# The expert stage of a diffusion layer: weights in whole-row chunks through twelve raw homes, products ordered gate, down of the neighbour, up

## The chip, the cores and the metric

The kernel runs on one core of a Trainium2 chip. The metric is the time of one execution on the device, in microseconds (us). The TensorE clock has two levels here, 1.2 and 2.4 GHz; the profile gives the granted clock as a share of the higher one.

## The reference, cut to what matters

One layer: a recurrent (RG-LRU) mixer over 1024 latent and 256 context tokens of width 1024, then a mixture of 16 experts where each expert chooses its 128 best tokens. The change touches the experts alone:

```python
xg = jax.vmap(lambda hb, ib: hb[ib])(h, idx)                    # 16 experts x 128 chosen rows x 1024
hid = jax.nn.silu(jnp.einsum('becd,edf->becf', xg, w_gate)) * jnp.einsum('becd,edf->becf', xg, w_up)
y = jnp.einsum('becf,efd->becd', hid, w_down) * gate[..., None].astype(h.dtype)   # f = 2048
return jax.vmap(lambda yb, ib: jnp.zeros((n, dm), yb.dtype).at[ib.reshape(-1)].add(yb.reshape(-1, dm)))(y, idx)
```

Everything is float32. Each expert's three weight matrices have 8 MB each, so 24 MB are read per expert, 384 MB in all, and each is used for 128 rows only.

## The kernel before, in words

The program is written out by hand for each engine, with semaphores between them. It has three stages: the mixer, the routing (output projection, softmax, top 128 of each expert), and the experts, which this document is about.

A float32 product is made of three: both operands are split into a rounded high part and the rest, the low part, and TensorE (PE) adds high times high, low times high and high times low. So each chunk of weights goes through a chain. SyncE (SP) loads it into a `raw` home of 1 MB (`load_chunk`). ScalarE (ACT) rounds it into `part_h` (`split` on ACT, recorded on the line of its helper `copy`, L498). VectorE (DVE) subtracts to get `part_l` (`split` on DVE, L980). PE does 12 matmuls of 128 columns of weights by 512 (L1218 to L1220 for gate and up, L1244 to L1246 for down), and `chunk_used` counts the chunks it has finished.

An expert has 24 chunks, with NS = 6 homes each for raw, high and low. The list `order` gives their sequence: two chunks of the neighbour's last down quarter, then for each quarter f of the 2048 hidden columns gate, gate, up, up, and behind them the two down chunks of quarter f-1. A gate or up chunk is four blocks of rows by 512 of the 2048 columns, so each partition gets four pieces of 2 KB; a down chunk is two pieces of 4 KB. `load_chunk` waits until the high and low parts of the chunk six earlier are made; ACT's `split` waits until PE has used the chunk six earlier.

For each quarter ACT takes silu of the gate product (`hidden`), DVE multiplies it by the up product into `hid` (`gate_up`, L987), PE transposes it (`turn_hidden`, L1228), and ACT and DVE split the transposed rows (`hidT_h`, `hidT_l` L991). Between experts PE transposes the next 128 rows (`turn_rows`, L1259), ACT scales and splits them (L683, L498), DVE makes `xgT_l` (L1009). DVE writes the expert's output `y_out` (L1000). GpSimd (POOL) scatters `y_out` with an adding DMA, then gathers the rows of the next expert. Each engine takes its instructions strictly in the written order, so one that waits holds all behind it.

Of the kernel before, what the change touches and what calls it, by code (L numbers as in the profile page):

```python
# [33 lines left out]
def program(nc, stack, x, c, ctx, c_ctx, ada_w, ada_b, norm_mix_g, norm_ffn_g, final_g, a_w_in, a_conv_w,  # L34
            a_conv_b, a_gate_wa, a_gate_ba, a_gate_wx, a_gate_bx, a_lambda, a_w_out, router_w,
            exp_w_gate, exp_w_up, exp_w_down, out):
    P = 128
# [99 lines left out]
    gate5_row = place("gate5_row", [P, D], F32, 195)  # L137
# [7 lines left out]
    NS = 6  # L145
    part_h = [place(f"part_h{s}", [P, 4 * HALF], F32R, 16 * s) for s in range(NS)]
    part_l = [place(f"part_l{s}", [P, 4 * HALF], F32R, 16 * s + 8) for s in range(NS)]
    raw = [place(f"raw{s}", [P, 4 * HALF], F32, 96 + 8 * s) for s in range(NS)]
    xg = place("xg", [P, D], F32, 146)
    xgT = place("xgT", [P, KD, P], F32, 150)  # L150
    xgT_h = place("xgT_h", [P, KD, P], F32R, 154)
    xgT_l = place("xgT_l", [P, KD, P], F32R, 158)
    act_g = [place(f"act_g{s}", [P, HALF], F32, 162 + 2 * s) for s in range(2)]
    hid = [place(f"hid{s}", [P, HALF], F32, 176 + 2 * s) for s in range(2)]
    hidT_h = [place(f"hidT_h{s}", [P, 4, P], F32R, 180 + 4 * s) for s in range(2)]
    hidT_l = [place(f"hidT_l{s}", [P, 4, P], F32R, 182 + 4 * s) for s in range(2)]
    y_out = place("y_out", [P, D], F32, 188)
# [24 lines left out]
    wg_v = exp_w_gate[0].rearrange("e (k p) f -> e p k f", p=P)  # L182
    wu_v = exp_w_up[0].rearrange("e (k p) f -> e p k f", p=P)
    wd_v = exp_w_down[0].rearrange("e (k p) f -> e p k f", p=P)
# [17 lines left out]
    raw_loaded = [stack.enter_context(nc.semaphore(f"raw_loaded{i}")) for i in range(NS)]  # L202
# [3 lines left out]
    fin_loaded = [stack.enter_context(nc.semaphore(f"fin_loaded{t}")) for t in range(NT)]  # L206
# [31 lines left out]
    order = [("d", 3, 0), ("d", 3, 1)]  # L238
    for f in range(NF):
        order += [("g", f, 0), ("g", f, 1), ("u", f, 0), ("u", f, 1)]  # L240
        if f:
            order += [("d", f - 1, 0), ("d", f - 1, 1)]
    CH = len(order)
    assert CH % NS == 0
    at = {key: i for i, key in enumerate(order)}

    used = lambda e, key: e * CH + at[key] - 1

    gate_at = lambda e, f: used(e, ("g", f, 1))
    up_at = lambda e, f: used(e, ("u", f, 1))  # L250
    down_at = lambda e, f: used(e + 1 if f == NF - 1 else e, ("d", f, 1))
    two_before = lambda e, f: (e, f - 2) if f >= 2 else (e - 1, f - 2 + NF)
# [6 lines left out]
    with nc.Block() as block:  # L259
# [3 lines left out]
        def _(sp):  # L263
# [108 lines left out]
            def load_chunk(e, i, first=False):  # L372
                kind, f, half = order[i]
                slot = i % NS
                if kind == "d":
                    e_of = e - 1 if f == NF - 1 else e
                    src = wd_v[bass.ds(e_of, 1), :, 4 * f + 2 * half:4 * f + 2 * half + 2, :]
                    dst = raw[slot][:].rearrange("p (k f) -> p k f", k=2)
                else:
                    src = (wg_v if kind == "g" else wu_v)[bass.ds(e, 1), :, 4 * half:4 * half + 4, f * HALF:(f + 1) * HALF]  # L380
                    dst = raw[slot][:].rearrange("p (k f) -> p k f", k=4)
                if not first:
# [8 lines left out]
            for i in range(2, 2 + NS):  # L391
                load_chunk(0, i, first=True)
            for t in range(NT - 2, NT):
                tile_stores(t, t % 2)

            for i in range(2 + NS, CH):
                load_chunk(0, i)
            with sp.Fori(1, E) as e:
                for i in range(CH):
                    load_chunk(e, i)  # L400

            for i in range(2):
                load_chunk(E, i)


            sp.wait_ge(sem["chunk_used"], E * CH)
            sp.dma_start(fin_g[:], row_of(final_g)).then_inc(sem["fin_g_loaded"], 16)
            sp.wait_ge(sem["scattered"], 16 * E)
            for t in range(NT):
                sp.dma_start(fin_in[:, t, :], x_scr[t * P:(t + 1) * P, :]).then_inc(fin_loaded[t], 16)  # L410
# [10 lines left out]
        def _(pool):  # L421
# [27 lines left out]
            for i in range(2, 2 + NS):  # L449
                slot = i % NS  # L450
                pool.wait_ge(sem["part_h_ready"], i - 1)
                nc.gpsimd.tensor_tensor(part_l[slot][:], raw[slot][:], part_h[slot][:].bitcast(F32), ALU.subtract
                                        ).then_inc(sem["part_l_ready"], 1)


# [28 lines left out]
            scatter(0, 1)  # L484
            with pool.Fori(1, E - 1) as e:
                pool.wait_ge(sem["gathered"], (e + 1) * 16)
                pool.wait_ge(sem["xgT_h_ready"], e + 1)
                gather(e + 1, sem["id_ready"], e + 1)
                scatter(e, e + 1)
# [6 lines left out]
        def _(act):  # L496
# [149 lines left out]
            def split(e, key):  # L646
                i = at[key]
                slot = i % NS
                uses = 0 if slot < 2 else 16
                act.wait_ge(raw_loaded[slot], e * (CH // NS * 16) + (i // NS) * 16 + uses)  # L650
                if not (isinstance(e, int) and e == 0 and i < 2 + NS):
                    act.wait_ge(sem["chunk_used"], e * CH + i - NS - 1)
                copy(part_h[slot][:], raw[slot][:]).then_inc(sem["part_h_ready"], 1)


            act.wait_ge(sem["gated_done"], 2 * NT)
            for key in order[2:2 + NS]:
                split(0, key)

            def hidden(e, f):  # L660

                act.wait_ge(sem["chunk_used"], gate_at(e, f))
                if not (isinstance(e, int) and e == 0 and f < 2):
                    act.wait_ge(sem["hid_ready"], e * NF + f - 1)
                nc.scalar.activation(act_g[f % 2][:], bank(2 * (f % 2)), ACT.Silu).then_inc(sem["silu_done"], 1)

            def turn_hidden(e, f):
                act.wait_ge(sem["hid_turned"], e * NF + f + 1)
                if not (isinstance(e, int) and e == 0 and f < 2):
                    act.wait_ge(sem["chunk_used"], down_at(*two_before(e, f)))  # L670
                copy(hidT_h[f % 2][:], bank(4 + f % 2)).then_inc(sem["hidT_h_ready"], 1)

            def expert(e, first=False):
                if not first:
                    split(e, ("d", 3, 0))
                    split(e, ("d", 3, 1))
                    turn_hidden(e - 1, 3)
# [10 lines left out]
                if not first:  # L688
                    act.wait_ge(sem["chunk_used"], up_at(e - 1, NF - 1))
                copy(xgT_h[:], xgT[:]).then_inc(sem["xgT_h_ready"], 1)  # L690
                for f in range(NF):
                    for key in (("g", f, 0), ("g", f, 1), ("u", f, 0), ("u", f, 1)):
                        if not (first and at[key] < 2 + NS):
                            split(e, key)
# [616 lines left out]
```

## Time and profile before

| | before |
|---|---|
| median of 3 runs | 1926.0 us (1923.76 to 1926.67) |
| the profiled execution | 1920.49 us, its span 1918.7 us |
| PE, VectorE, ScalarE busy, share of the span | 85%, 72%, 63% |
| granted TensorE clock, mean | 0.938 |
| moved by DMA | 511.08 MB, mean 266 GB/s |

How its rows are read. A row of the timeline has the start in us from the span's start, the duration in us, engine, line, operation, output<-inputs, shapes, the count of merged instructions, and in brackets the idle time of the engine before it with what ended it. A row of a table of windows has the stretch, its length, the busy us and instructions of PE, PEld (weight loads), DVE, ACT and POOL, then the granted clock, the busy share of the 16 DMA engines (a little over 1 where packets overlap), and GB/s. A row of waits has who waited on whom, the total, how often, and the longest. A queue's row has packets, MB, and the share of 16 engines' time that its packets took; q1 carries the loads of SP, q0 the gathers and scatters. A row of loads by line has the issue's min/median/max in ns, or the us from issue to landing.

### The profile page before, as it was taken

How to read it: one execution, taken by the hardware profiler on the slowest of the kernel's cores; microseconds unless marked ns; L12 is line 12 of the kernel's file. 1: busy time of each engine (PE TensorE's matmuls, PEld its weight loads, DVE VectorE, ACT ScalarE, POOL GpSimd, SP SyncE). 2: the span in 40 equal slices, each digit the busy share in tenths (PEclk: the TensorE clock that was granted, in tenths of full speed). 3: DMA queues.
4: the chain of work that ended last, by engine and by line, in shares of the span. 5: the costliest groups of instructions: out<-in, count | busy, mean ns of one | idle time of the engine just before them, and what ended most of it. 6: DMA issues, size and time to landing. Idle time of an engine off the chain costs nothing.

```text
span 1918.7 us, 21818 instructions
## 1 busy us (share of the span) xinstructions
PE 1638.6 (85%) x7524; PEld 1318.5 (69%) x7524; DVE 1388.0 (72%) x1044; ACT 1206.3 (63%) x1141; POOL 108.5 (6%) x125
## 2 busy tenths in 40 slices
PE   4999999946992098998989989989899899898992
PEld 1777777835882077877877777778777777787772
DVE  3778778764225757878878878788878788887784
ACT  4687887880224056767666667666675676666763
POOL 0300000000005000000000000000000000000000
PEclk7999999977995599999999999999999999999996
DMA  8234343324583159999999999999999999999995
GB/s 325 72 111 147 116 141 118 127 67 154 181 273 111 53 206 328 383 337 342 366 321 340 360 325 376 326 331 364 340 342 350 327 353 352 331 358 332 340 332 197
DMA packets 238469, 511.08 MB, mean 266 GB/s; under 512 B 10298, under 2 KB 56024, under 8 KB 236384
## 3 DMA queue, kind: packets, MB, share of 16 engines
q1 hardware_dynamic: 230944, 483.33, 70.0%
q0 software_dynamic: 7488, 27.27, 4.9%
q8 instruction: 22, 0.36, 0.1%
q14 instruction: 15, 0.12, 0.0%
HBM read 479.10 MB, written 31.46 MB: 266 GB/s over the span
## 4 chain that ended last, share of the span: by engine, by line
PE 76%; DVE 10%; ACT 7%; issue 2%; SPq 2%; DMA 2%; ACTq 0%; DVEq 0%; POOL 0%; POOLq 0%
PE psum L1218 13%; PE psum L1220 12%; PE psum L1219 12%; PE psum L1046 5%; PE psum L1048 5%; PE psum L1047 5%; PE psum L1244 5%; PE psum L1245 4%; PE psum L1246 4%; DVE part_l L980 4%; ACT xgT L683 2%; PE psum L1146 2%; PE psum L1147 2%; PE psum L1148 2%; ACT part_h L498 1%
## 5 line engine op out<-in xcount | busy, mean ns | idle before, releaser
L980 DVE TENSOR_TENSOR part_l<-raw,part_h 128x2048 fp32r<-128x2048 f32 x378 | 843.3, 2287 | 85.4 <-ACT part_h L498 85.4
L498 ACT ACTIVATE part_h<-raw 128x2048 fp32r<-128x2048 f32 x384 | 700.7, 1908 | 0.7 <-DMA raw<-in_exp_w_up_dram 0.7
L1218 PE MATMUL psum<-part_h,xgT_h 128*128 128x512 f32 x1024 | 415.6, 406 | 73.3 <-DVE part_l L980 68.7
L1219 PE MATMUL psum<-part_h,xgT_l 128*128 128x512 f32 x1024 | 406.3, 397 | 0.0
L1220 PE MATMUL psum<-part_l,xgT_h 128*128 128x512 f32 x1024 | 405.7, 396 | 0.0
L1218 PEld LDWEIGHTS psum<-part_h,xgT_h 128*128 128x128 f32 x1024 | 197.0, 192 | 125.5 <-DVE part_l L980 81.4
L498 ACT ACTIVATE hidT_h<-psum 128x512 fp32r<-128x512 f32 x64 | 38.3, 598 | 341.7 <-PE psum L1228 341.7
L1220 PEld LDWEIGHTS psum<-part_l,xgT_h 128*128 128x128 f32 x1024 | 196.8, 192 | 43.0
L1219 PEld LDWEIGHTS psum<-part_h,xgT_l 128*128 128x128 f32 x1024 | 197.5, 193 | 39.3
L1244 PE MATMUL psum<-part_h,hidT_h 128*128 128x512 f32 x512 | 206.2, 403 | 13.8 <-DVE hidT_l L991 13.8
L1245 PE MATMUL psum<-part_h,hidT_l 128*128 128x512 f32 x512 | 200.0, 391 | 0.0
L1246 PE MATMUL psum<-part_l,hidT_h 128*128 128x512 f32 x512 | 199.8, 390 | 0.0
L1244 PEld LDWEIGHTS psum<-part_h,hidT_h 128*128 128x128 f32 x512 | 96.0, 188 | 49.1 <-DVE part_l L980 28.0
L1246 PEld LDWEIGHTS psum<-part_l,hidT_h 128*128 128x128 f32 x512 | 96.1, 188 | 20.9
L1245 PEld LDWEIGHTS psum<-part_h,hidT_l 128*128 128x128 f32 x512 | 96.2, 188 | 18.1
L1146 PE MATMUL psum<-act_h,yt_h 128*128 128x512 f32 x156 | 62.1, 398 | 42.2 <-DVE act_l L854 42.2
L987 DVE TENSOR_TENSOR hid<-act_g,psum 128x512 f32<-128x512 f32 x64 | 43.7, 683 | 65.6 <-PE psum L1220 65.6
L683 ACT ACTIVATE xgT<-psum,shift,scale 128x128 f32<-128x128 f32 x128 | 46.3, 474 | 61.0 <-PE psum L1259 61.0
L1046 PE MATMUL psum<-act_h,wu_h 128*128 128x512 f32 (+1 forms) x224 | 78.8, 352 | 1.5 <-DVE act_l L796 1.5
L991 DVE TENSOR_TENSOR hidT_l<-psum,hidT_h 128x512 fp32r<-128x512 f32 x64 | 44.2, 690 | 48.0 <-ACT hidT_h L498 48.0
L1047 PE MATMUL psum<-act_h,wu_l 128*128 128x512 f32 (+1 forms) x224 | 78.7, 351 | 0.0
L1048 PE MATMUL psum<-act_l,wu_h 128*128 128x512 f32 (+1 forms) x224 | 78.6, 351 | 0.0
(199 smaller groups left out, 2134.6 us busy)
## 6 DMA issues: line engine op xcount, KB each, us to landing
raw<-in_exp_w_gate_dram SPq DMA_DIRECT2D x128, 1024.0 KB, 7.3
raw<-in_exp_w_up_dram SPq DMA_DIRECT2D x128, 1024.0 KB, 7.0
raw<-in_exp_w_down_dram SPq DMA_DIRECT2D x128, 1024.0 KB, 6.2
ada_piece<-in_ada_w_dram SPq DMA_DIRECT2D x16, 1024.0 KB, 6.6
ada_buf<-in_ada_w_dram SPq DMA_DIRECT2D x8, 1024.0 KB, 13.0
u_raw<-in_a_w_in_dram SPq DMA_DIRECT2D x10, 512.0 KB, 3.8
g_raw<-in_a_w_in_dram SPq DMA_DIRECT2D x10, 512.0 KB, 8.4
y_scr<-y_h POOLq DMA_DIRECT2D x10, 512.0 KB, 2.9
```

What stands on the lines that cost most here:

```text
L498: return nc.scalar.activation(dst, src, ACT.Identity)
L980: v.tensor_tensor(part_l[slot][:], raw[slot][:], part_h[slot][:].bitcast(F32), ALU.subtract).then_inc(sem["part_l_ready"], 1)
L1046: mm(out_ap, xh, wh, start=(i == 0), stop=False)
L1047: mm(out_ap, xl, wh, start=False, stop=False)
L1048: last = mm(out_ap, xh, wl, start=False, stop=(i == len(pairs) - 1))
L1146: mm(out_ap, yh, wo_h[:, n, cols], start=(n == 0), stop=False)
L1218: mm(dst, xgT_h[:, kk, :], wh[:, k, :], start=(kk == 0), stop=False)
L1219: mm(dst, xgT_l[:, kk, :], wh[:, k, :], start=False, stop=False)
L1220: last = mm(dst, xgT_h[:, kk, :], wl[:, k, :], start=False, stop=(kk == KD - 1))
L1244: mm(bank(6 + n), hidT_h[f % 2][:, kk, :], wh[:, k, cols], start=first, stop=False)
L1245: mm(bank(6 + n), hidT_l[f % 2][:, kk, :], wh[:, k, cols], start=False, stop=False)
L1246: last = mm(bank(6 + n), hidT_h[f % 2][:, kk, :], wl[:, k, cols], start=False, stop=final)
```

## The change

Chunks become whole rows. A gate or up chunk i is now rows 128i to 128i+127 over all 2048 columns, and a down chunk is 256 rows by 1024 with two adjacent rows per partition, so each partition gets one piece of 8 KB. There are still 24 chunks of 1 MB and 12 matmuls per chunk. Raw and low share twelve homes (`part_l` is written over its raw home); six homes hold the high parts. A home is reloaded when PE has used the chunk twelve earlier.

The order per expert e is gate chunks 0 to 7 of e, down chunks 0 to 7 of e-1, up chunks 0 to 7 of e. Gate accumulates in four PSUM banks at once, up and down in the other four. PE waits for the high part first, uses it eight times, and only then waits for the low part. All four quarters of `hid` are multiplied, turned and split together, in the gate phase of the next expert. The rows of the next expert are turned after up chunk 3, into a second pair of homes for `xgT_h` and `xgT_l`. POOL gathers ahead of the scatter. Since down columns are paired, `turn_hidden` reads `hid` with a step of two elements.

```diff
-    NS = 6
-    part_h = [place(f"part_h{s}", [P, 4 * HALF], F32R, 16 * s) for s in range(NS)]
+    NR, NH_W = 12, 6
+    raw_kb = [88 + 8 * s for s in range(7)] + [40 + 8 * s for s in range(5)]
+    part_h = [place(f"part_h{s}", [P, FF], F32R, kb) for s, kb in enumerate((0, 8, 16, 24, 32, 80))]
+    part_l = [place(f"part_l{s}", [P, FF], F32R, kb) for s, kb in enumerate(raw_kb)]
+    raw = [place(f"raw{s}", [P, FF], F32, kb) for s, kb in enumerate(raw_kb)]
...
-    wg_v = exp_w_gate[0].rearrange("e (k p) f -> e p k f", p=P)
-    wd_v = exp_w_down[0].rearrange("e (k p) f -> e p k f", p=P)
+    wg_v = exp_w_gate[0].rearrange("e (k p) f -> e k p f", p=P)
+    wd_v = exp_w_down[0].rearrange("e (k p r) f -> e k p (r f)", p=P, r=2)
...
-                    sp.wait_ge(sem["part_h_ready"], e * CH + i - NS - 1)
-                    sp.wait_ge(sem["part_l_ready"], e * CH + i - NS - 1)
-                sp.dma_start(dst, src.rearrange("o p k f -> (o p) k f")).then_inc(raw_loaded[slot], 16)
+                wait_past(sp, sem["chunk_used"], chunk(e, kind, i, first) - NR + 1)
+                sp.dma_start(raw[slot][:], src[bass.ds(e, 1), i].rearrange("o p f -> (o p) f")).then_inc(raw_loaded[slot], 16)
...
+            def expert(e, slot):
+                for i in range(CHUNKS):
+                    split(e, "g", i)
+                    if i == 0:
+                        gathered_rows(e, slot)
+                    if i == 6:
+                        turn_hidden(e - 1)
+                for i in range(CHUNKS):
+                    split(e - 1, "d", i)
+                    if i == 4:
+                        gated(e)
+                for i in range(CHUNKS):
+                    split(e, "u", i)
...
+            def expert(e, slot, before_first=False):
+                for i in range(CHUNKS):
+                    split(e, "g", i)
+                    if i == 0:
+                        gathered_rows(e, slot)
+                    if i == 4:
+                        gate_up(e - 1, before_first)
+                    if i == 7:
+                        turn_hidden(e - 1)
+                for i in range(CHUNKS):
+                    split(e - 1, "d", i)
+                for i in range(CHUNKS):
+                    split(e, "u", i)
+                    if i == 3:
+                        expert_out(e - 1)
...
+            def ups(e, slot, first=False, last=False):
+                up_start(e, slot, first)
+                for i in range(2, CHUNKS):
+                    up_product(e, i, slot, first)
+                    if i == 3 and not last:
+                        turn_rows(e + 1)
+
+            def expert(e, slot, last=False):
+                for i in range(CHUNKS):
+                    gate_product(e, i, slot)
+                    if i in (1, 2):
+                        turn_hidden(e - 1, 2 * i - 2)
+                        turn_hidden(e - 1, 2 * i - 1)
+                downs(e - 1)
+                ups(e, slot, last=last)
```

`up_start` does the upper two banks of up chunks 0 and 1 first, then waits for `y_ready` (the down output lies in the lower two), then does the lower two.

Two places of the written order matter most. The first is on PE, at the head of an expert in the loop. Before (`hid_160` is the last quarter of the neighbour, `xg` the gathered rows, `part_l_141` the low part in home 0):

```order
L1228 MATMUL psum<-ident,hid_160 128x128 [waits hid_ready]
L1228 MATMUL psum<-ident,hid_160 128x128 x3
L1253 ISA
L1256 ISA [waits gathered]
L1259 MATMUL psum<-ident,xg 128x128 [waits hid_ready]
L1259 MATMUL psum<-ident,xg 128x128 x7
L1238 ISA [waits hidT_l_ready]
L1244 MATMUL psum<-part_h_135,hidT_h_162 128x512 [waits part_l_ready]
L1245 MATMUL psum<-part_h_135,hidT_l_164 128x512
L1246 MATMUL psum<-part_l_141,hidT_h_162 128x512
```

In the change, at the same place of an expert (two gate chunks in; `hid` is the whole hidden row of the neighbour, `part_h_135` high home 0):

```order
L1223 MATMUL psum<-part_l_146,xgT_h_168 128x512 [waits part_l_ready]
L1223 MATMUL psum<-part_l_146,xgT_h_168 128x512 x3
L1251 ISA
L1254 MATMUL psum<-ident,hid 128x128 [waits hid_ready]
L1254 MATMUL psum<-ident,hid 128x128 x3
L1251 REGISTER_ALU
L1254 MATMUL psum<-ident,hid 128x128 [waits hid_ready]
L1254 MATMUL psum<-ident,hid 128x128 x3
L1213 REGISTER_ALU
L1215 MATMUL psum<-part_h_135,xgT_h_168 128x512 [waits part_h_ready]
```

What moved: the turns of the hidden rows have a gate chunk ahead of them and one behind, and the wait for `hidT_l` no longer follows them directly; the turn of the gathered rows has left this place.

The second is on DVE, around the product of gate and up. Before, in quarter 0 of an expert:

```order
L980 TENSOR_TENSOR part_l_145<-raw_151,part_h_139 128x2048 [waits part_h_ready]
L979 REGISTER_ALU
L980 TENSOR_TENSOR part_l_146<-raw_152,part_h_140 128x2048 [waits part_h_ready]
L257 REGISTER_ALU [waits chunk_used]
L1000 REGISTER_ALU [waits scattered]
L1000 SCALAR_TENSOR_TENSOR y_out<-psum,gate_v,gate_row 128x512 x2
L983 ISA
L986 REGISTER_ALU [waits chunk_used,silu_done]
L987 TENSOR_TENSOR hid_159<-act_g_157,psum 128x512 [waits hid_turned]
```

In the change, in the gate phase of the next expert (`part_l_149` is gate chunk 4):

```order
L975 TENSOR_TENSOR part_l_148<-raw_160,part_h_136 128x2048 [waits part_h_ready]
L974 REGISTER_ALU
L975 TENSOR_TENSOR part_l_149<-raw_161,part_h_137 128x2048 [waits part_h_ready]
L978 ISA
L982 TENSOR_TENSOR hid<-hid,psum 128x512 [waits chunk_used,silu_done]
L982 TENSOR_TENSOR hid<-hid,psum 128x512 x3
L974 REGISTER_ALU
L975 TENSOR_TENSOR part_l_150<-raw_162,part_h_138 128x2048 [waits part_h_ready]
L974 REGISTER_ALU
L975 TENSOR_TENSOR part_l_151<-raw_163,part_h_139 128x2048 [waits part_h_ready]
L975 TENSOR_TENSOR part_l_152<-raw_164,part_h_140 128x2048 [waits part_h_ready]
```

What moved: before, the multiply waits for an up product whose chunks were split directly ahead of it, and the next gate chunk's split stands behind it. In the change it waits for the up product of the expert before, with five splits of the next gate chunks already ahead of it.

## Rows read from the trace of the kernel before

**Rows 1.** Table of windows: the expert stage, from 740 to 1886 us.

```profile
740.00:1886.00 1146.00, 1063.27 (x4696) 858.25 (x4696) 914.56 (x527) 772.67 (x614) 43.48 (x58) 0.98 0.94 339
```

**Rows 2.** Timeline: first matmul of the stage, two scatters, last output.

```profile
674.37 0.79 PE L1218 MATMUL psum<-part_h,xgT_h 128*128 128x512 f32 x1 [4.58 <-DVE xgT_l L1009]
...
755.45 0.18 POOL L470 COPY id_scatter<-tok_id 128x1 int32<-128x1 int32 x1 [79.33 <-DVE y_out L1000]
...
1819.96 0.18 POOL L470 COPY id_scatter<-tok_id 128x1 int32 x1 [71.78 <-DVE y_out L1000]
...
1885.34 1.41 DVE L1000 SCALAR_TENSOR_TENSOR y_out<-psum,gate_v,gate_row 128x512 f32<-128x512 f32 x2 [5.87 <-PE psum L1246]
```

**Rows 3.** Waits of PE, 740 to 1886 us: total, times, longest.

```profile
PE psum L1218 <- DVE part_l L980: 68.7, 30, 3.1
PE psum L1244 <- DVE hidT_l L991: 13.8, 16, 1.6
```

**Rows 4.** Timeline of PE at the three gaps of one expert.

```profile
1347.34 0.49 PE L1244 MATMUL psum<-part_h,hidT_h 128*128 128x512 f32 x1 [0.79 <-DVE hidT_l L991]
...
1354.54 0.50 PE L1218 MATMUL psum<-part_h,xgT_h 128*128 128x512 f32 x1 [1.47 <-DVE part_l L980]
...
1365.33 0.39 PE L1220 MATMUL psum<-part_l,xgT_h 128*128 128x512 f32 x1
1368.86 0.50 PE L1218 MATMUL psum<-part_h,xgT_h 128*128 128x512 f32 x1 [3.14 <-DVE part_l L980]
```

**Rows 5.** Timeline of ScalarE and VectorE in the same expert.

```profile
1346.29 2.90 ACT L683 ACTIVATE xgT<-psum,shift,scale 128x128 f32<-128x128 f32 x8
1350.26 7.31 ACT L498 ACTIVATE part_h<-raw 128x2048 fp32r<-128x2048 f32 x4
1350.38 1.23 DVE L1009 TENSOR_TENSOR xgT_l<-xgT,xgT_h 128x1024 fp32r<-128x1024 f32 x1 [3.17 <-ACT xgT_h L498]
1352.19 8.90 DVE L980 TENSOR_TENSOR part_l<-raw,part_h 128x2048 fp32r<-128x2048 f32 x4 [0.58 <-ACT part_h L498]
1361.01 1.41 DVE L1000 SCALAR_TENSOR_TENSOR y_out<-psum,gate_v,gate_row 128x512 f32<-128x512 f32 x2
1365.91 0.69 DVE L987 TENSOR_TENSOR hid<-act_g,psum 128x512 f32<-128x512 f32 x1 [3.50 <-PE psum L1220]
```

**Rows 6.** Timeline of PE in two stretches without a gap.

```profile
684.40 0.39 PE L1218 MATMUL psum<-part_h,xgT_h 128*128 128x512 f32 x1
...
692.33 0.39 PE L1220 MATMUL psum<-part_l,xgT_h 128*128 128x512 f32 x1
...
1316.40 0.39 PE L1220 MATMUL psum<-part_l,xgT_h 128*128 128x512 f32 x1
1316.64 0.60 PE L1228 MATMUL psum<-ident,hid 128*128 128x128 f32 x4
1317.31 0.40 PE L1219 MATMUL psum<-part_h,xgT_l 128*128 128x512 f32 x1
```

**Rows 7.** DMA queues, 1300 to 1376 us: packets, MB, share.

```profile
q1 hardware_dynamic: 10689, 25.30, 91.1%
q0 software_dynamic: 288, 1.05, 5.3%
```

**Rows 8.** Table of windows: program's start, and three inside one expert.

```profile
10.00:20.00 10.00, 6.91 (x32) 0.60 (x24) 2.96 (x17) 1.69 (x3) 0.00 (x0) 1.00 1.02 425
1300.00:1305.00 5.00, 5.00 (x25) 4.15 (x23) 2.42 (x2) 4.65 (x5) 0.00 (x0) 1.00 1.04 397
1325.00:1330.00 5.00, 5.00 (x24) 4.14 (x23) 5.00 (x4) 4.18 (x3) 0.00 (x0) 1.00 1.02 405
1352.00:1358.00 6.00, 4.53 (x20) 3.45 (x19) 5.81 (x3) 5.57 (x4) 0.00 (x0) 1.00 0.52 166
```

**Rows 9.** Loads by line: issue time of ada_buf, landing of expert loads.

```profile
L268 SPq DMA_DIRECT2D ada_buf<-in_ada_w_dram x8: 359/448/659, 4.4 to 9.4; - x8
...
DMA to landing us min/median/max: 4.8/6.8/14.1
```

More of the change, by code:

```diff
@@ L143, in program @@
     top_idf = place("top_idf", [E, CAP], F32, 175)
[L145 to L157 removed]
+    NR, NH_W = 12, 6
[3 more added lines that the diff above has]
+    raw = [place(f"raw{s}", [P, FF], F32, kb) for s, kb in enumerate(raw_kb)]
+    xg = place("xg", [P, D], F32, 144)
+    xgT = place("xgT", [P, KD, P], F32, 148)
+    xgT_h = [place(f"xgT_h{s}", [P, KD, P], F32R, 152 + 4 * s) for s in range(2)]
+    xgT_l = [place(f"xgT_l{s}", [P, KD, P], F32R, 160 + 4 * s) for s in range(2)]
+    hid = place("hid", [P, FF], F32, 168)
+    hidT_h = place("hidT_h", [P, FF // P, P], F32R, 176)
+    hidT_l = place("hidT_l", [P, FF // P, P], F32R, 184)
+    y_out = place("y_out", [P, D], F32, 192)
     fin_in = place("fin_in", [P, NT, D], F32, 0)
@@ new lines, in _, with gated @@
+            act.wait_ge(sem["gated_done"], 2 * NT)
+            for i in range(EARLY):
+                split(0, "g", i, first=True)
+            def gated(e, first=False):
+                act.wait_ge(sem["chunk_used"], chunk(e, "g", CHUNKS - 1, first) + 1)
+                if not first:
+                    act.wait_ge(sem["hid_turned"], e * NF)
+                for f in range(NF):
+                    nc.scalar.activation(hid[:, f * HALF:(f + 1) * HALF], bank(f), ACT.Silu).then_inc(sem["silu_done"], 1)
@@ L687, in expert @@
                 act.wait_ge(sem["xgT_ready"], e * 2 + 2)
[L688 to L694, printed above, removed]
-                    if f:
-                        turn_hidden(e, f - 1)
-                    hidden(e, f)
-                    if f:
-                        split(e, ("d", f - 1, 0))
-                        split(e, ("d", f - 1, 1))
@@ new lines, in _ @@
+            gathered_rows(0, 0)
+            for i in range(EARLY, CHUNKS):
+                split(0, "g", i, first=True)
+            for i in range(CHUNKS):
+                split(0, "u", i, first=True)
+                if i == 4:
+                    gated(0, first=True)
+            expert(1, 1)
+            with act.Fori(1, E // 2) as j:
+                expert(j * 2, 0)
+                expert(j * 2 + 1, 1)
+            for i in range(CHUNKS):
+                split(E - 1, "d", i)
+                if i == 4:
+                    turn_hidden(E - 1)
@@ new lines, in _ @@
+            gathered_rows(0, 0)
+            for i in range(EARLY, CHUNKS):
+                split(0, "g", i, first=True)
+            for i in range(CHUNKS):
+                split(0, "u", i, first=True)
+            expert(1, 1, before_first=True)
+            with dve.Fori(1, E // 2) as j:
+                expert(j * 2, 0)
+                expert(j * 2 + 1, 1)
+            for i in range(CHUNKS):
+                split(E - 1, "d", i)
+                if i == 4:
+                    gate_up(E - 1)
+                    turn_hidden(E - 1)
@@ new lines, in weights, with in_high @@
+                return r(part_h[high_slot(e, kind, i, first)]), r(part_l[raw_slot(e, kind, i, first)])
+            def in_high(e, kind, i, slot, cols, first=False):
+                wh, wl = weights(e, kind, i, first)
+                pe.wait_ge(sem["part_h_ready"], chunk(e, kind, i, first) + 1)
+                for f, dst in cols:
+                    mm(dst, xgT_h[slot][:, i, :], wh[:, f, :], start=(i == 0), stop=False)
+                for f, dst in cols:
+                    mm(dst, xgT_l[slot][:, i, :], wh[:, f, :], start=False, stop=False)
```

329 lines of the change are left out of this document (148 added, 181 removed).

## The prediction

> **What bounds the kernel now.** I read the table of windows first. In the 1146 us from 740 to 1886 PE was busy for 1063, VectorE for 915, ScalarE for 773, the DMA engines for 94%, and the mean clock was 0.98 [rows 1]. Everything is close to full, so what matters is who waits for whom. The stage runs from the first matmul at 674.37 to the last output at 1885.34, 1211.0 us, and the scatter numbers of experts 0 and 14 lie 1064.5 us apart, 76.04 us per expert [rows 2].
>
> The waits of PE name two causes: 68.7 us in 30 waits for `part_l`, two per expert, and 13.8 us in 16 for `hidT_l` [rows 3]. Their sum, 82.5, is all of PE's idle time in that window (1146 less 1063.3). One expert shows where they stand: 0.79, 1.47 and 3.14 us [rows 4]. The other engines say why. ScalarE turns the gathered rows at 1346.29 and only then splits the first gate chunk, at 1350.26. VectorE sits 3.17 us in front of `xgT_l`, then makes four low parts in 8.90 us. Then it stands 3.50 us in front of `hid`, which needs PE's up product, while the next gate chunk's split is queued behind [rows 5]. PE ends that product at 1365.33 and waits for just that split [rows 4, 5]. So the stage is bound by PE plus a hand-over at each expert's head, not by a DMA or by VectorE's total.
>
> PE's floor: from 684.40 to 692.33 there are 35 steps of one matmul, 0.2266 us each. From 1316.40 to 1317.31 there are two such steps and four transposes, so one transpose adds (0.91 - 0.453) / 4 = 0.114 us [rows 6]. The stage has 16 x 288 = 4608 matmuls and 256 + 120 transposes after its first matmul: 1044.2 + 42.9 = 1087 us, 68.0 per expert. The stage takes 124 us more: 82.5 are waits, about 23 are the clock (2% of 1146), the rest of some 18 is in steps a little over 0.2266 that no row assigns.
>
> **The change part by part.**
>
> *The order (removes the hand-over).* Matmul and transpose counts stay, so PE's 1087 stay. I follow one expert with T = 0 at the end of the previous up chunk 7 and PE never waiting: a chunk is 12 x 0.2266 = 2.72 us, a group of four transposes 0.46; gate ends at 23.5, down at 45.3, up at 68.0. ScalarE needs 7.31 / 4 = 1.83 us per split, VectorE 8.90 / 4 = 2.22 [rows 5], and ScalarE may run six chunks ahead of PE.
> - Gathered rows: PE turns them after up chunk 3, at -10.9; ScalarE needs 2.9 + 1.06, VectorE has `xgT_l` by about -5.5. PE wants it at 0.
> - `hid`: VectorE has split gate chunks 0 to 4 by 3.7 (the last was allowed when up chunk 6 was used, at -2.7, behind ScalarE's queue), then four multiplies of about 0.65 (0.69 for one alone [rows 5]): the first is out at 4.4. PE wants it at 5.4 after gate chunk 1. Slack 1.0 us.
> - `hidT`: turned by 9.9, rounded by ScalarE by 10.4 (it holds gate split 7 back to 12.2, wanted at 20.8), split by VectorE by 16.9, wanted at 23.5.
> - silu: gate is done at 23.5, ScalarE takes 2.4, its next split (down 5) is ready at 27.4 and wanted at 37.
> - `y_out`: down ends at 45.3, VectorE's queue is empty by 43.9, two writes of 1.41 together [rows 5] end at 46.7. PE wants them at 48.1, since `up_start` puts half of two chunks ahead. Slack 1.4 us.
> - VectorE's total is 24 x 2.22 + 8 x 0.65 + 1.4 + 1.2 = 61 us of 68; ScalarE's is less.
>
> No wait is left on PE. The waits removed are 82.5 us; with no gap before it the clock should hold, another 23. So the gain from waits and clock is 105, and down to the floor of 1087 it is 124. Both bounds stay in the range; I take 115, between them, since no row says whether the 18 us go with the waits.
>
> *The end.* The last expert's down now has nothing to lie behind. VectorE's split of down chunk 4 comes before the multiplies and ends 1.5 us after up chunk 7; then four multiplies (to 4.1), turn and rounding of the last quarter, and the low parts by 6.6. Less the four turn groups (1.8, already counted) PE idles 4.8 us, against 1.6 for the last of the 16 waits now [rows 3]. Cost 3, and 2 to 4 more if the clock falls in that gap (it fell to 0.98 on average around gaps of 3.14). I take 6.
>
> *Transposes of `hid` with a step of two.* No row has a strided weight load. Below, nothing; above, 0.114 us more for each of 256 (twice the present price), 29 us. The nearest row is the plain transpose and the count of elements is the same, so I take nothing.
>
> *Two waits per chunk, matmuls that rotate over four banks.* The weight loads stay one per matmul. At nothing: the low part comes 2.2 us after the high one, both a chunk or more early. SP issues a load in 0.4 to 0.7 us where rows are 8 KB [rows 9], of 2.85 between loads.
>
> *Gather ahead of scatter.* Now and then the gathered rows are not waited for by PE after expert 0; no row of PE's waits names a DMA [rows 3]. Nothing. If the cover were gone, it would cost one landing, about 7 us per expert [rows 9].
>
> *Whole rows and twelve homes (the DMA).* This is the part that can take the gain back. At 68.5 us per expert the core must move its 26.35 MB (25.30 + 1.05 in 76 us [rows 7]) at 385 GB/s, more than it does now. Today 24.13 loads of 1.0486 MB took 91.1% of 76 us, 2.87 us each, and q0 5.3%, 0.17 per chunk [rows 7]: 3.04. With 8 KB per partition (`ada_buf` at the program's start) full engines moved 425 GB/s, with gate and up rows of 2 KB 397, with down rows of 4 KB 405 [rows 8]. So a load goes from 2.87 to about 2.87 x 397 / 425 = 2.68, and with q0 2.85 us per chunk. At the best, 1.0486 / 0.425 + 0.17 = 2.64. PE's pace over the stage is (1087 + 9) / 384 = 2.85. The two are even; twelve homes give a load some 30 us between issue and use, where six gave bursts and then idle engines (0.52 busy and 166 GB/s from 1352 to 1358 [rows 8]). The first 12 chunks are there before the stage as they are now (6 split, 6 raw). The DMA alone would end the stage after 372 x 2.85 + 15 (landing, two splits, the last matmuls) = 1075. I take no loss.
>
> The Trainium skill ("DMA: Bandwidth & Descriptors", Specifications) gives an HBM limit of about 358 GB/s per core. By that rule an expert could not take less than 26.35 / 0.358 = 73.6 us and the stage would come to about 1157 us. The windows of 397, 405 and 425 GB/s lie above it, so the trace disagrees while the other core of the pair is idle.
>
> **The sum.** 115 - 6 = 109 us off the profiled execution's 1920.5: 1811.5. The median of the runs shown lies 5.5 above that execution, so I give 1816.
>
> **The rivals.**
> 1. *The DMA binds.* If packets gain nothing from being whole, a chunk costs 3.04: 372 x 3.04 + 15 = 1146, the stage gains 65 and the time is 1861. For it: the engines are 94% busy already. Against it: the 425 GB/s, and idle engines at the head. The page's 358 GB/s would give 1157, thus 1872, by the same mechanism.
> 2. *New waits take the place of the old.* The slacks of 1.0 and 1.4 us are thin. If VectorE runs 2.5 us later than I worked out, PE waits 1.5 before the first turn and 1.1 before the lower up banks, 2.6 x 15 = 39 us, and the clock falls again as now, 23: 1878; with one of the two, 1840. For it: VectorE is busy 61 of 68. Against it: it has ten chunks' slack elsewhere to catch up in.
> 3. *Slower than before.* Packets of 8 KB under the stage's load are slower than short ones, one mechanism at one place, the loads. The stage is as long as now when a chunk costs (1211 - 15) / 372 = 3.21 us, so a load 3.04, 345 GB/s. At 330 it is 3.18 + 0.17, 372 x 3.35 + 15 = 1261: 1976. For it only that nothing in the stage has such packets yet; against it the 425.
> 4. *It doesn't do what it says:* the gather moved ahead buys nothing by itself. If the other waits stayed too, 1926.
>
> **How the numbers follow.** Forecast (1796 to 1835) 0.63; the DMA binds at some rate (1835 to 1875) 0.17; new waits (1835 to 1880) 0.12; slower than before 0.04; no difference 0.01; below 1796 (rotating banks make the step shorter) 0.03. The range from 1796 to 1865 takes in the forecast and most of the two next, and the strided transposes' 29 us. What a measurement of this kernel can tell from no change is about 0.2%, 4 us. Faster 0.95, same 0.01, slower 0.04.
>
> **What would show it.** Right: an interval of 68 to 69.5 us per expert, no wait of PE over 0.5 us inside the stage but one of 4 to 6 at its end, the clock at 1.00 through the stage, q1 at 380 GB/s or more and landings under 15 us. The DMA rival: landings of 20 us and more, ScalarE waiting for DMAs, the engines at 1.0 all along. The waits rival: rows of PE waiting for `hid` or `y_out`. The strided turn: transposes over 0.114 apart. Wrong altogether if a load takes over 3.04 us.

## The result, and the profile after

The changed kernel takes 1808.53 us (median of 4 runs, 1807.69 to 1809.96), the kernel before 1926.34 in the same session (4 runs, 1923.76 to 1927.24). The ratio is 0.9391, with a 95% interval from 0.9375 to 0.9408: 6.1% faster. The forecast was 1816, in a range from 1796 to 1865. The profiled execution took 1807.95 us, 112.5 less than that of before.

The table of windows of the changed kernel, for the stage and for 100 us inside it; it answers to [rows 1, 8].

```profile
740.00:1770.00 1030.00, 1026.31 (x4680) 854.17 (x4679) 908.27 (x524) 783.82 (x603) 125.22 (x56) 1.00 0.95 372
1200.00:1300.00 100.00, 100.00 (x461) 83.42 (x460) 90.17 (x55) 77.31 (x61) 8.88 (x4) 1.00 0.99 393
```

PE is never idle between 1200 and 1300, its clock is full, and the DMA engines move 393 GB/s. ("DMA: Bandwidth & Descriptors" of the Trainium skill gives about 358 GB/s per core, in its Specifications; this window, with one core running, disagrees, as those of before did.)

The timeline of the changed kernel: first matmul, two scatters in a row, last output, as in [rows 2].

```profile
674.33 2.08 PE L1215 MATMUL psum<-part_h,xgT_h 128*128 128x512 f32 x4 [4.58 <-DVE xgT_l L1000]
...
1245.46 2.08 POOL L462 COPY id_scatter<-tok_id 128x1 int32 x1 [49.62 <-DVE y_out L995]
...
1313.64 2.08 POOL L462 COPY id_scatter<-tok_id 128x1 int32 x1 [49.62 <-DVE y_out L995]
...
1773.37 1.41 DVE L995 SCALAR_TENSOR_TENSOR y_out<-psum,gate_v,gate_row 128x512 f32<-128x512 f32 x2 [12.02 <-PE psum L1274]
```

From the first matmul to the last output it is 1099.0 us where it was 1211.0, and 68.18 us per expert where it was 76.04. All of the gain is in this stage.

PE's waits in the changed kernel from 740 to 1790 us (total, times, longest), against [rows 3]:

```profile
PE psum L1254 <- DVE hid L982: 2.3, 1, 2.3
PE psum L1267 <- DVE hidT_l L987: 1.4, 1, 1.4
```

All 46 waits are gone, and these two stand at the last expert's end. Then VectorE and PE at the head of an expert in the changed kernel (their timelines), against [rows 4, 5]:

```profile
1312.07 1.41 DVE L995 SCALAR_TENSOR_TENSOR y_out<-psum,gate_v,gate_row 128x512 f32<-128x512 f32 x2 [1.39 <-PE psum L1274]
...
1327.22 1.23 DVE L1000 TENSOR_TENSOR xgT_l<-xgT,xgT_h 128x1024 fp32r<-128x1024 f32 x1 [2.61 <-ACT xgT_h L490]
1329.03 8.90 DVE L975 TENSOR_TENSOR part_l<-raw,part_h 128x2048 fp32r<-128x2048 f32 x4 [0.58 <-ACT part_h L490]
1337.84 2.47 DVE L982 TENSOR_TENSOR hid<-hid,psum 128x512 f32<-128x512 f32 x4
1340.23 4.49 DVE L975 TENSOR_TENSOR part_l<-raw,part_h 128x2048 fp32r<-128x2048 f32 x2
```

```profile
1338.87 1.08 PE L1223 MATMUL psum<-part_l,xgT_h 128*128 128x512 f32 x4
1339.78 1.11 PE L1254 MATMUL psum<-ident,hid 128*128 128x128 f32 x8
1340.65 1.17 PE L1215 MATMUL psum<-part_h,xgT_h 128*128 128x512 f32 x4
```

VectorE no longer stands in front of `hid`. It comes to the multiplies at 1337.84, and the first of the four is out about 0.62 later, at 1338.5. PE starts the turn at 1339.78 without waiting, as late as its own queue brings it there: 1.3 us of slack.

The DMA view of the changed kernel from 1300 to 1369 us: the queues (packets, MB, share), and loads with their median us to landing, as in [rows 7]:

```profile
q1 hardware_dynamic: 3492, 25.44, 91.7%
q0 software_dynamic: 288, 1.05, 5.7%
...
raw<-in_exp_w_up_dram SPq DMA_DIRECT2D x8, 1024.0 KB, 5.2
raw<-in_exp_w_gate_dram SPq DMA_DIRECT2D x8, 1024.0 KB, 4.8
raw<-in_exp_w_down_dram SPq DMA_DIRECT2D x8, 1024.0 KB, 9.0
```

The same bytes as in 76 us before go in 69 us, with a third of the packets, at the same share of the engines' time.

Against the prediction's signs of being right: the interval of 68.18 us, the clock of 1.00 and the missing waits are there. Two signs are not. The loads' queue moves 25.44 MB in 69 us, 369 GB/s where 380 was asked, and the longest landing is 19.3 us, not under 15 (median 6.9). No wait of PE comes from either.

### The profile page after: what moved, and what is told of

Its sections match the earlier page's. It is cut to its first block, busy times and chain, and to the rows that moved or that the text cites. A ratio compares the mean times of both kernels' runs of the same rounds, so it can differ in the third digit from the quotient of the medians.

```text
span 1806.2 us, 21028 instructions
## 1 busy us (share of the span) xinstructions
PE 1605.9 (89%) x7524; PEld 1318.7 (73%) x7524; DVE 1385.8 (77%) x1044; ACT 1227.8 (68%) x1141; POOL 194.2 (11%) x125
## 4 chain that ended last, share of the span: by engine, by line
PE 85%; DVE 7%; ACT 4%; SPq 2%; DMA 1%; issue 1%; POOL 0%; ACTq 0%; DVEq 0%; POOLq 0%
PE psum L1215 13%; PE psum L1217 13%; PE psum L1223 13%; PE psum L1267 6%; PE psum L1269 6%; PE psum L1274 6%; PE psum L1050 5%; PE psum L1051 5%; PE psum L1052 5%; PE psum L1150 2%; PE psum L1151 2%; PE psum L1152 2%; PE psum L1254 2%; SPq L274 1%; DVE top_id L962 1%; DVE top_val L960 1%
## 5 line engine op out<-in xcount | busy, mean ns | idle before, releaser
L490 ACT ACTIVATE part_h<-raw 128x2048 fp32r<-128x2048 f32 x384 | 720.7, 1917 | 158.2 <-PE psum L1223 82.3
L1215 PE MATMUL psum<-part_h,xgT_h 128*128 128x512 f32 x1024 | 284.4, 395 | 4.6 <-DVE xgT_l L1000 4.6
L1217 PE MATMUL psum<-part_h,xgT_l 128*128 128x512 f32 x1024 | 280.0, 390 | 0.0
L1223 PE MATMUL psum<-part_l,xgT_h 128*128 128x512 f32 x1024 | 279.8, 390 | 0.0
L1267 PE MATMUL psum<-part_h,hidT_h 128*128 128x512 f32 x512 | 158.7, 391 | 1.4 <-DVE hidT_l L987 1.4
L1269 PE MATMUL psum<-part_h,hidT_l 128*128 128x512 f32 x512 | 158.5, 391 | 0.0
L1274 PE MATMUL psum<-part_l,hidT_h 128*128 128x512 f32 x512 | 137.1, 390 | 0.0
L462 POOL COPY id_scatter<-tok_id 128x1 int32 (+1 forms) x16 | 31.4, 1965 | 803.5 <-DVE y_out L995 803.5
L606 ACT ACTIVATE xn<-x 128x1024 f32<-128x1024 f32 x8 | 8.5, 1060 | 105.7 <-DVE x L913 105.7
L911 DVE TENSOR_TENSOR x<-psum,gate_row 128x512 f32<-128x512 f32 x16 | 11.1, 692 | 87.9 <-PE psum L1152 87.9
```

The source lines that it names most:

```text
L490: return nc.scalar.activation(dst, src, ACT.Identity)
L1215: mm(dst, xgT_h[slot][:, i, :], wh[:, f, :], start=(i == 0), stop=False)
L1217: mm(dst, xgT_l[slot][:, i, :], wh[:, f, :], start=False, stop=False)
L1223: last = mm(dst, xgT_h[slot][:, i, :], wl[:, f, :], start=False, stop=(i == CHUNKS - 1))
L1267: mm(bank(4 + n), hh, wh[:, k, cols], start=(i == 0 and k == 0), stop=False)
L1269: mm(bank(4 + n), hl, wh[:, k, cols], start=False, stop=False)
```

## The experiments

Each kernel ran beside the kernel before on the same chip. Unless said otherwise the edit is to the changed kernel, whose 1808.5 us is the mark.

**Short pieces again.** Gate and up chunks are once more four blocks of rows by 512 columns (pieces of 2 KB), down chunks two pieces of 4 KB; the transposes of `hid` have no step. Order of the phases and homes stay. Two things go along with it: each gate or up chunk now goes to one bank instead of four in turn, and the first two up chunks lie whole in the upper banks, so PE has two chunks of cover in front of `y_ready` where it had one chunk's worth.

```diff
-    wg_v = exp_w_gate[0].rearrange("e (k p) f -> e k p f", p=P)
-    wd_v = exp_w_down[0].rearrange("e (k p r) f -> e k p (r f)", p=P, r=2)
+    wg_v = exp_w_gate[0].rearrange("e (j k p) (f c) -> e j f p k c", p=P, j=2, c=HALF)
+    wd_v = exp_w_down[0].rearrange("e (k r p) f -> e k p r f", p=P, r=2)
...
```

> The changed kernel, with the loads cut into short pieces as before: gate and up chunks of four pieces of 2 KB per partition, down chunks of two pieces of 4 KB; homes, order and matmul count are those of the change (the four blocks of a chunk go to one bank, and the transposes of hid have no step). Theory (whole rows are what keeps the loads level with TensorE): a chunk costs the DMA engines 3.04 us with q0, against TensorE's 2.84, so the stage comes to about 1146 us instead of 1099, 1855 us in all, landings rise to 20 us and more, and the engines' share goes to 1.0. Rival (the pieces do not matter, order and homes do it): within 4 us of 1808.5, landings as in the changed kernel.

Measured: 1807.27 us (1806.45 to 1808.17), ratio to before 0.9389 (0.9373 to 0.9404). The window of its stage, one of 76 us inside it, and from the DMA view of the same 76 us the loads' queue:

```profile
740.00:1770.00 1030.00, 1026.31 (x4690) 852.18 (x4689) 908.38 (x524) 786.95 (x604) 125.23 (x56) 1.00 1.01 373
1300.00:1376.00 76.00, 76.00 (x349) 63.15 (x348) 68.60 (x39) 58.60 (x45) 8.89 (x4) 1.00 1.04 384
```

```profile
q1 hardware_dynamic: 12129, 28.15, 98.2%
```

My theory fell. In the same 76 us the changed kernel has 3848 packets in this queue, so 3.2 times the packets carry the same 384 GB/s, and PE is as busy to the hundredth. Landings stay as they were (median 6.9, longest 14.2 us). What changed is the share, 1.01 in place of 0.95 over the stage and 1.04 in place of 0.98 over the 76 us, without any effect on the time. So the share of packet time does not tell how much room is left, and a cost per load made from it is not a cost.

One limit of this: 384 GB/s is what PE's pace asks for in both kernels, not the most that either can carry. Single slices of about 1.9 us reach 412 GB/s with short pieces and 444 with whole rows. Whole rows may be faster at the top; this kernel doesn't need it.

**Only the down rows** in 4 KB pieces, transposes without a step.

```diff
-                    lo = (2 * f + k // 2) * 2 * P + k % 2
-                    ... hid[:, lo:lo + 2 * P - 1:2], ident[:])
+                    lo = (4 * f + k) * P
+                    ... hid[:, lo:lo + P], ident[:])
```

> The changed kernel, with down chunks alone in two pieces of 4 KB per partition, so that hid is transposed without a step. Theory: loads cost (16 x 2.60 + 8 x 2.75) / 24 + 0.16 = 2.81 us per chunk, still under TensorE's 2.84, and a weight load with a step of two costs nothing: 1808 within 3 us, the turns' spacing unchanged. Rival (the step costs): faster by up to 29 us, each turn 0.114 us shorter.

Measured: 1807.02 us (1805.23 to 1807.79), ratio 0.9389. The times can't tell a cost of the step, but the trace can. PE at the first turn of an expert without the step:

```profile
1338.55 1.04 PE L1258 MATMUL psum<-ident,hid 128*128 128x128 f32 x8
1339.34 1.17 PE L1219 MATMUL psum<-part_h,xgT_h 128*128 128x512 f32 x4
```

Eight transposes take 0.79 us here. With the step they take 0.87 (1339.78 to 1340.65 in the changed kernel, shown above), where the gathered rows, transposed without a step in that same kernel, take 0.79 (1322.57 to 1323.36). The scatters lie 68.01 us apart where they were 68.18; with short pieces they lie 68.0 apart too. So the step costs about 0.01 us per transpose, an estimated 2.6 us in all: not the 29 of the rival, and within the 3 us of my theory, but not nothing.

**Eight and six raw homes** in place of twelve.

```diff
-    NR, NH_W = 12, 6
+    NR, NH_W = 8, 6        # and 6, 6
...
```

With six, the loads ahead of the stage stop at six as well.

> The changed kernel with eight raw homes in place of twelve. With six homes the run before this one took 80.3 us per expert, 6 chunks in 20.1 us: issue, landing, rounding, low part, use, and what ScalarE does between. Theory (the loop of a home is about 20 us long, and the stage stalls when homes x TensorE's 2.84 us is less): eight homes give 22.7 us, so they nearly suffice, 1808 to 1830 us, with ScalarE waiting for loads only behind the scatter and gather. Rival (each home fewer costs in proportion, 194 us for six): a third of the way back, 1930 us.

> The changed kernel with six raw homes in place of twelve. A load is then issued six chunks ahead, 5 x 2.84 = 14.2 us before its use, of which issue, rounding and low part take 4.6, so 9.6 are left for the landing, whose median is 6.9 and longest 19.3 in the changed kernel. Theory (homes are a cushion, the order is what counts): waits only behind the scatter and the gather, 1 to 3 us per expert, 1825 to 1855 us with the clock. Rival (twelve homes are the gain): back to 1900 and more.

Measured with eight: 1823.62 us (1822.15 to 1825.57), ratio 0.9469 (0.9453 to 0.9485), as expected; the one new wait of PE is for `hid`, 13.6 us in 10 waits. With six: 2002.53 us (1999.96 to 2004.84), ratio 1.0407 (1.0389 to 1.0424), slower than before. Waits with six homes, ScalarE's first, then PE's, from 740 to 1985 us, and the window of its stage:

```profile
ACT part_h L491 <- DMA raw<-in_exp_w_up_dram: 159.4, 114, 7.3
ACT part_h L491 <- DMA raw<-in_exp_w_down_dram: 111.1, 96, 8.9
ACT part_h L491 <- DMA raw<-in_exp_w_gate_dram: 83.3, 30, 4.4
```

```profile
PE psum L1255 <- DVE hid L983: 62.8, 15, 10.5
PE psum L1216 <- DVE y_out L996: 38.8, 15, 3.5
PE psum L1216 <- DVE xgT_l L1001: 23.1, 14, 2.9
```

```profile
740.00:1970.00 1230.00, 1098.96 (x4730) 898.07 (x4728) 927.48 (x531) 794.69 (x607) 127.60 (x58) 0.95 0.84 319
```

My theory of the six homes fell. ScalarE waits 354 us for loads while the DMA engines are 0.84 busy: the loads start too late. Before, six homes did, since a raw home was free once it was split. Now the low part lies in it until PE has used the chunk. Landing 4.8, split 1.9, low part 2.3 and products 2.7 are 11.7 us, less than the 16.3 that PE takes for six chunks, so in steady running six homes should do, and they do. The loss is at the hand-overs. Two windows of this kernel, one behind PE's wait for `hid` and one in the down phase:

```profile
1296.00:1301.00 5.00, 5.00 (x16) 4.11 (x16) 5.00 (x3) 2.84 (x3) 0.00 (x0) 0.58 0.07 28
1305.00:1337.00 32.00, 32.00 (x143) 26.50 (x142) 27.73 (x16) 22.85 (x15) 0.00 (x0) 1.00 0.96 373
```

In the down phase PE is never idle and the loads run at 373 GB/s. At the head of the expert PE waits 4.26 us for `hid` (to 1294.86), runs slowly behind it (clock 0.58), and frees no home, so SP issues no load from 1290.76 to 1301.39, and the engines move 28 GB/s. It is the same behind `y_out`: `up_start` frees neither of its two chunks before `y_ready`, and no load is issued from 1337.61 to 1344.41. Each stop of PE thus stops the loads, which holds up the splits that PE needs next. That this loop makes up the whole loss is read from the one expert; no run tests it alone.

**One split moved, in the kernel before.** VectorE splits the next gate chunk ahead of the multiply of quarter 0, nothing else.

```diff
-                        if not (first and at[key] < 2 + NS):
+                        if not (first and at[key] < 2 + NS) and not (f == 1 and key == ("g", 1, 0)):
...
+                        split(e, ("g", 1, 0))
```

> The kernel before, with one edit on VectorE: in experts 1 to 15 the low part of the first chunk of gate quarter 1 is made ahead of the multiply of quarter 0, which waits for TensorE's up product. Theory (the hand-over at an expert's head is what the old order loses): the gap of 3.14 us goes, 15 x 3.14 = 47 us, and part of the clock's 23 with it: 1856 to 1879 us. Rival (TensorE then waits for something else there, loads or ScalarE): less than 15 us gained, a wait of about 3 us at the same place with another releaser.

Measured: 1863.08 us (1862.15 to 1864.31), ratio 0.9681 (0.9664 to 0.9697). PE's waits, for [rows 3]:

```profile
PE psum L1219 <- DVE part_l L980: 28.0, 30, 1.5
PE psum L1245 <- DVE hidT_l L991: 13.9, 16, 1.6
```

The gap of 3.14 is down to a few tenths, and 40.6 us of waits are gone. The time fell by 61.6, so 21.0 come from elsewhere, and most of that is the clock. It is at 1.00 in this kernel's stage. In the kernel before, six of the 14 intervals between scatters are 74.8 us long, and eight are 76.4 or 77.5 us, with the clock below 1.00: some 17 us together. Nearly all of the clock's loss hung on that one gap. The hand-over theory holds, and one line of order in the old layout gives half of the whole change. Which parts of the new order remove the other 41.9 us of waits was not tried one by one.

**The scatter ahead of the gather**, as before the change.

```diff
+                scatter(e - 2, e - 1)
                 gather(e, sem["id_ready"], e)
-                scatter(e - 2, e - 1)
```

> The changed kernel with GpSimd's old order, the scatter of an expert ahead of the gather. Theory (the gather ahead gains nothing itself but the new order needs it): the gather is then issued after the scatter, 10 us behind y_out, and lands some 7 to 10 us later, 64 to 68 us into the expert, where TensorE wants the rows at 56: a wait of 8 to 12 us in 14 experts, 1920 to 1980 us. Rival (the gathered rows come early enough anyway, as in the kernel before): within 4 us of 1808.5.

Measured: 1999.23 us (1998.85 to 2001.1), ratio 1.0386 (1.0369 to 1.0404), slower than before and above what I expected. The timeline of POOL and PE at one expert:

```profile
1340.76 2.08 POOL L462 COPY id_scatter<-tok_id 128x1 int32 x1 [72.21 <-DVE y_out L995]
1343.66 2.81 POOL L465 DMA_INDIRECT x_scr<-y_out,id_scatter  x1 [0.82 <-POOL id_scatter L462]
1345.91 1.46 POOL L452 COPY id_gather<-tok_id 128x1 int32 x1
1348.17 2.24 POOL L455 DMA_INDIRECT xg<-n_scr,id_gather  x1 [0.79 <-POOL id_gather L452]
```

```profile
1360.86 1.97 PE L1284 MATMUL psum<-ident,xg 128*128 128x128 f32 x8 [11.01 <-DMA xg<-n_scr,id_gather]
1362.47 2.06 PE L1215 MATMUL psum<-part_h,xgT_h 128*128 128x512 f32 x4
```

The gather is issued at 1348.17 and PE wants its rows at 1349.85. It waits 11.01 us, then works at half clock (2.06 for four matmuls in place of 1.07). An expert takes 81.9 us, 13.7 more: 11.0 of wait and 2.7 of clock. So the gather ahead is no detail. PE now turns the rows in the middle of the up phase and wants them 9.3 us after `y_out` is written (1340.60), but behind the scatter the gather needs 7.6 us to be issued and 12.6 to land. In the changed kernel, free of the scatter, it is issued at 1329.29 for a turn at 1390.74, 61 us ahead.

**The upper banks of two up chunks not done first** (`up_start` becomes two plain `up_product`).

> The changed kernel without the split start of up: TensorE waits for y_ready before up chunk 0. Theory (the half chunks ahead cover the two writes of y_out): a wait of 1.5 us per expert, 15 x 1.5 = 22 us, 1831 us, clock unchanged. Rival (cover not needed, or the stall lets other engines run ahead and is given back): within 5 us of 1808.5.

Measured: 1839.96 us (1838.61 to 1843.45), ratio 0.9562 (0.9545 to 0.9578). PE's wait:

```profile
PE psum L1215 <- DVE y_out L995: 26.1, 15, 1.8
```

1.74 us each time. `up_start` gives 12 matmuls, 2.72 us, of cover, so the slack of `y_out` is 1.0 us. The time is 31.4 above the mark, the waits are 26.1: each costs 0.35 more than its row says.

**The multiplies two splits later** (`if i == 6` for `if i == 4` on VectorE).

> The changed kernel with VectorE's four multiplies two splits later, behind gate chunk 6. Theory (the place of the multiply decides, slack 1.2 us in the changed kernel): hid comes 4.5 us later, TensorE waits 3.3 us at the first turn in 15 experts, 50 us, and the clock falls at gaps of that length as before the change, up to 23: 1858 to 1882 us. Rival (gates ahead absorb it): under 20 us.

Measured: 1868.07 us (1867.7 to 1872.76), ratio 0.9702 (0.9686 to 0.9718). PE's wait:

```profile
PE psum L1254 <- DVE hid L982: 45.1, 15, 3.1
```

Two splits are 4.45 us and the wait is 3.0 to 3.1, so 1.4 of slack were used up first, where the timeline shows 1.3. The time is 59.5 above the mark for 45.1 of waits: the clock is at 0.99 from 740 to 1800, so it falls behind some of these gaps.

**Another tail, and a control.** The last expert's multiplies and low parts of the turned rows go quarter by quarter, ahead of VectorE's split of down chunk 4; its down product lies in the gate's two lower banks and begins when the first quarter is turned and split.

```diff
+            dve.wait_ge(sem["chunk_used"], chunk(E - 1, "u", CHUNKS - 1) + 1)
+            multiply(0)
+            multiply(1)
+            low_hidden(E - 1, 0)
...
+            for i in range(4, CHUNKS):
+                split(E - 1, "d", i)
+            expert_out(E - 1, 0)
...
+            turn_hidden(E - 1, 0)
+            turn_hidden(E - 1, 1)
+            down_product(E - 1, 0, at=0)
```

> The changed kernel idles PE 3.7 us behind the last up product (2.3 for hid, 1.4 for hidT_l), and the clock is at half for 6.8 us after it, which costs 3.4. Here the last expert's four multiplies come before VectorE's split of down chunk 4, each low part of the turned rows follows its quarter, and PE starts down chunk 0 (in the gate's two lower banks) when the first quarter of the turned rows is split. Theory (the end idles for VectorE's queue, and the clock falls for that gap): PE idles at most 2 us there in pieces, the clock may hold, and the time is 1803 to 1806.5 where the changed kernel has 1808.5, ratio to it 0.997 to 0.999. Rival (the end is bound by the chain multiply, turn, round, subtract and not by its place in the queue, or the clock falls anyway): the idle pieces add to 3 us or more and the time is within 1.5 us of the changed kernel's.

> The changed kernel once more, unedited, on the same chip as the kernel with the other tail: 1807.5 to 1810 us. It is there so that a difference of two or three us can be read within one chip.

Measured: 1804.88 us (5 runs, 1804.62 to 1805.36) against 1808.95 for the control (5 runs, 1808.08 to 1809.24), whose runs lie all above; 4.1 us, 0.23%. Against before the ratio is 0.9371 (0.9358 to 0.9383). PE at the end of the control, then at the end with the new tail:

```profile
1745.23 3.00 PE L1254 MATMUL psum<-ident,hid 128*128 128x128 f32 x16 [2.27 <-DVE hid L982]
1749.64 1.22 PE L1267 MATMUL psum<-part_h,hidT_h 128*128 128x512 f32 x2 [1.41 <-DVE hidT_l L987]
1750.66 1.05 PE L1269 MATMUL psum<-part_h,hidT_l 128*128 128x512 f32 x2
```

```profile
1744.20 1.34 PE L1269 MATMUL psum<-ident,hid 128*128 128x128 f32 x8 [0.85 <-DVE hid L985]
1746.35 0.73 PE L1284 MATMUL psum<-part_h,hidT_h 128*128 128x512 f32 x2 [0.81 <-DVE hidT_l L989]
1746.92 0.63 PE L1286 MATMUL psum<-part_h,hidT_l 128*128 128x512 f32 x2
```

The idle time fell from 3.7 to 1.7 us, and two matmuls take 0.63 right behind it where the control's take 1.05 at half clock. From 1740 to 1775 us the clock is 0.99, in the control 0.90. This is the fastest kernel of the study.

## Why the prediction was right, and where its steps were off

**What bounds the kernel: right.** A stage bound by PE plus a hand-over at each expert's head: the moved split alone gives 61.6 of 118 us, and with the whole order PE is 100.00 busy of 100.

**The order: right, and the slacks nearly so.** `hid` was said to have 1.0 us and has 1.3 to 1.4; `y_out` 1.4 and has 1.0. The late multiply and the missing `up_start` show that both are real and thin, which was the ground of the rival of new waits; it did not come.

**The sum: 7.5 us too high as given.** 1811.5 and 5.5 are 1817, not 1816, so the sum as it stands is 8.5 above the measured time. Of these, 4.9 are no part of the kernel: I added the 5.5 by which the median of before lay above its profiled execution, and after the change the two lie 0.6 apart (1808.53 and 1807.95). The other 3.5 are the gain, 112.5 between the profiled executions where I had 109.

**The gain from the order: a little too small.** I took 115 and left open whether 18 us more go with the waits. The stage lost 112.0, and its end cost about 5.5 more than before (below), so the order gave about 117.5: with the 105 of waits and clock, some 12 of the 18 went. Taking the middle of 105 and 124 was a guess that came close, not a reckoning. The rows of before can say why, had I looked behind the gaps:

```profile
1352.68 0.39 PE L1246 MATMUL psum<-part_l,hidT_h 128*128 128x512 f32 x1
1354.54 0.50 PE L1218 MATMUL psum<-part_h,xgT_h 128*128 128x512 f32 x1 [1.47 <-DVE part_l L980]
1354.88 0.39 PE L1219 MATMUL psum<-part_h,xgT_l 128*128 128x512 f32 x1
```

From 1352.68 to 1354.88 are 2.20 us for two steps of 0.2266, so this gap costs 1.75, and its row says 1.47. The idle time is counted from the modelled end of the last matmul (0.39 behind its start, where the next could start 0.2266 behind it), and the first one after the gap is slow. A quarter of a us for each of three gaps in 16 experts is some 12 us, the size of what went. The kernel without `up_start` shows the same from the other side, 0.35 per wait. Of the stage's 1099.0 us the floor was to be 1087; the end's idle time and the clock behind it are 7.1, the first matmuls at the low clock (2.08 for four, where 1.07 is usual) about 1.8, and 68.18 - 67.94 = 0.24 per expert is left, 3. The transposes with a step are 0.17 of these 0.24.

**The end: right in kind, a little dear.** PE idles 3.7 us where I said 4.8, and the clock falls behind it as I feared: it is 0.66 from 1744 to 1754, as much as 6.8 us at half, which costs 3.4. Less the 1.6 that the end cost before, that is 5.5; I took 6. In the other tail, with shorter gaps, the clock holds.

**The DMA: right in its answer, wrong in its reckoning.** I made 3.04 and 2.85 us per chunk out of the queues' share of packet time, and called demand and supply even; the whole of the rival "the DMA binds" (0.17, 1861) stood on that. That the two came out even, and not against the change, was luck. Short pieces show that packets of 2 KB carry the same 384 GB/s at a share of 1.04. So the 94% of before, at 339 GB/s, was not a sign of full engines (the moved split alone brought the old layout to 360 GB/s over its stage), and the whole rows gain nothing here. Why the share comes out so high is not shown; packets in flight may count while they wait for one another. The rival that long packets are slower is out too: with 8 KB they carry what PE asks for, and no wait names a load.

**Twelve homes: under-priced.** I spoke of a cover of 30 us and gave no price for less. Eight homes cost 15 us, six 194.

**Gather ahead of scatter: wrong.** I took nothing, and about 7 us per expert without the cover, the landing of a load. The gather's own landing is 10.7 us in the changed kernel and 12.6 with the scatter first. I argued from the kernel before, where PE waits for no gather, and did not follow the scatter's and the gather's place in the new order. There the edit is worth 11.0 us of wait and 2.7 of clock per expert, 190.7 in all. The forecast was safe only because the change contains it.

**Transposes with a step, rotating banks, two waits per chunk.** The step costs an estimated 2.6 us where I took nothing; the sign I named is there, small as it is. Counted as the prediction counts the 0.114, with the matmuls around them taken off, the changed kernel's transposes with a step are 0.122 us apart (1338.87 to 1341.66) and those without 0.112 (1321.65 to 1324.36). Rotating banks cost nothing: with each chunk in one bank the interval is 68.0, as it is without the step and with rotating banks. Two waits per chunk were not tried alone; a gate chunk takes 2.72 us with them (1328.89 to 1331.61), the floor's value.

## What to carry to other kernels

Where a fast engine waits for a slow one at a hand-over, look at what the slow one has queued behind its own wait: moving one split ahead of a wait gave half of a large rewrite's gain. Price each home and each early issue of a new order in that order, by its own round trip and by what stops it at the hand-overs; in the order before it may be worth nothing. And don't work out room for transfers from the busy share of DMA engines: ask whether anyone waits for a landing.

## What the hardware did that I had not expected

- A share of DMA packet time over 1 (1.04 over 76 us) went with full speed and no wait of PE; single slices of that kernel moved 412 GB/s.
- POOL's small operations became slow in the new order: the copy of 128 indices takes 2.08 us where it took 0.18 [rows 2], and the issue of a scatter 2.81. Both fall in stretches where VectorE is splitting without a pause; that this is the cause was not tried. It is hidden, but it adds to the late gather's wait in the kernel with the scatter first.
- A gap of PE costs about 0.25 us more than its idle row says.
- At the end, the clock held behind gaps of 0.85 and 0.81 us, where 2.27 and 1.41 brought it to half. The length of one gap alone does not decide it: without `up_start` fifteen waits of 1.74 us left the stage at 1.00, and in the kernel before the same gap of 3.14 us was followed by steps of 0.23 us at 1368.86 and of 0.43 at 1443.66. What does decide it is open.
